# When VectorE scales the attention probabilities: behind the next projection's work, or ahead of it

## The reference

```python
def joint_softmax(parts, sink=None):
    ...
    es = [jnp.exp(s - m) for s in parts]
    den = es[0].sum(axis=-1, keepdims=True)
    ...
    if sink is not None:
        den = den + jnp.exp(sink - m)
    return [e / den for e in es]
```

```python
    hx = modulate(rmsnorm(x, g_pre_mix[l]), sh1, sc1)
    hc = modulate(rmsnorm(h_ctx, g_pre_mix[l]), csh1, csc1)
    y_x, y_c = mixer_sublayer(hx, hc, cos, sin, w_in[l], ...)
```

## Time and profile before

| | us |
|---|---|
| median of 3 runs | 2631.29 |
| lowest and highest | 2630.23, 2636.59 |
| the profiled execution's own time | 2638.48 |
| its span, first to last instruction | 2636.4 |
| PE busy | 2415.6 |
| DVE busy | 1743.0 |
| ACT busy | 1343.1 |
| mixer of layer 0, about | 37 to 740 |
| dense feed-forward, about | 740 to 1175 |
| mixer of layer 1, about | 1190 to 1560 |
| experts | from 1605 |

### The profile page before, as it was taken

How to read it: one execution, slowest core, us unless ns; L and a number is a source line. 1 busy time by engine, 2 the same in 40 slices (tenths; PEclk the granted TensorE clock), 3 DMA queues, 4 the chain that set the end, 5 groups by cost and what they waited for, 6 DMA issues and landing times.

```text
span 2636.4 us, 34852 instructions
## 1 busy us (share of the span) xinstructions
PE 2415.6 (92%) x12536; PEld 1970.1 (75%) x12536; DVE 1743.0 (66%) x2249; ACT 1343.1 (51%) x1636; POOL 28.1 (1%) x26
## 2 busy tenths in 40 slices
PE   6887899989889999987998978999999999999997
PEld 3666687667658788766887867787888888888885
DVE  5455434544275425547736638989989898989897
ACT  5334423433244323324534436777767676767675
POOL 0000010000000000000001000000000000000000
PEclk8988999989989999999999978999999999999999
DMA  5222132233324434322233436989899998989894
GB/s 218 80 80 96 69 107 89 88 106 119 112 80 159 143 112 160 135 88 79 98 104 118 152 127 264 357 337 361 338 353 343 353 338 337 361 329 365 327 366 171
DMA packets 128776, 528.62 MB, mean 201 GB/s; under 512 B 9136, under 2 KB 68016, under 8 KB 75440
## 3 DMA queue, kind: packets, MB, share of 16 engines
q1 hardware_dynamic: 126096, 520.86, 53.8%
q10 hardware_dynamic: 2592, 6.55, 0.8%
HBM read 526.33 MB, written 1.05 MB: 200 GB/s over the span
## 4 chain that ended last, share of the span: by engine, by line
PE 82%; DVE 10%; ACT 4%; issue 3%; DMA 1%; ACTq 0%; DVEq 0%; SPq 0%
PE O L1620 11%; PE pp L1277 9%; PE pp L1278 8%; PE pp L1279 8%; PE S L1598 8%; PE S L1596 8%; PE S L1597 8%; PE pp L1301 3%; DVE wsp L834 3%; PE O L1294 2%; PE T L1384 2%; ACT wsp L548 2%; PE S L1277 1%; PE S L1278 1%; PE T L1278 1%
## 5 line engine op out<-in xcount | busy, mean ns | idle before, releaser
L834 DVE TENSOR_TENSOR wsp<-raw,wsp 128x1024 fp32r<-128x1024 f32 (+3 forms) x344 | 379.4, 1127 | 523.0 <-ACT wsp L548 518.4
L1224 DVE TENSOR_TENSOR opr<-M,opr 128x2048 fp32r<-128x2048 f32 x168 | 383.5, 2287 | 31.1 <-ACT opr L782 28.3
L548 ACT ACTIVATE wsp<-raw 128x1024 fp32r<-128x1024 f32 (+3 forms) x344 | 322.5, 966 | 130.7 <-PE T L1279 82.3
L782 ACT ACTIVATE opr<-M 128x2048 fp32r<-128x2048 f32 x168 | 322.6, 1920 | 93.3 <-PE O L1620 52.0
L1596 PE MATMUL S<-opr,hx 128*128 128x512 f32 x896 | 359.5, 401 | 2.2 <-DVE hx L1229 2.2
L1598 PE MATMUL S<-opr,hx 128*128 128x512 f32 x896 | 350.7, 391 | 0.0
L1597 PE MATMUL S<-opr,hx 128*128 128x512 f32 x896 | 349.9, 391 | 0.0
L1620 PE MATMUL O<-opr,wsp 128*128 128x512 f32 x1344 | 311.3, 391 | 13.0 <-DVE opr L1224 13.0
L1277 PE MATMUL pp<-hx,wsp 128*128 128x512 f32 (+1 forms) x800 | 290.8, 363 | 35.4 <-DVE hx L916 14.8
L1620 PEld LDWEIGHTS O<-opr,wsp 128*128 128x128 f32 x1344 | 250.5, 188 | 67.6 <-DVE opr L1224 16.4
L1278 PE MATMUL pp<-hx,wsp 128*128 128x512 f32 (+1 forms) x800 | 283.5, 354 | 0.0
(11 more groups left out here) (203 smaller groups left out, 3422.6 us busy)
## 6 DMA issues: line engine op xcount, KB each, us to landing
M<-in_w_moe SPq DMA_DIRECT2D x168, 1024.0 KB, 4.9
raw<-in_w_main SPq DMA_DIRECT2D x132, 1024.0 KB, 4.9
raw<-in_w_moe SPq DMA_DIRECT2D x114, 1024.0 KB, 5.0
xm<-in_w_moe SPq DMA_DIRECT2D x56, 1024.0 KB, 5.7
raw<-in_w_br SPq DMA_DIRECT2D x24, 512.0 KB, 3.5
raw<-in_w_dn SPq DMA_DIRECT2D x8, 768.0 KB, 4.1
raw<-in_w_dn SPq DMA_DIRECT2D x8, 640.0 KB, 3.9
M<-in_rpb_rows ACTq DMA_DIRECT2D x16, 256.0 KB, 2.9
```

What stands on the lines that cost most here:

```text
L548: act.activation(wsp[:, slot, 0, 0:w], raw[:, slot // 2, half * w:half * w + w], ACT.Copy).then_inc(hi_done, 1)
L782: act.activation(wse[i % SPLIT_E][:, 0, :, :], raw_e[i % RAW_E], ACT.Copy).then_inc(e_hi, 1)
L834: dve.tensor_tensor(wsp[:, slot, 1, 0:w], raw[:, slot // 2, half * w:half * w + w], wsp[:, slot, 0, 0:w], ALU.subtract).then_inc(lo_done, 1)
L1224: dve.tensor_tensor(w[:, 1, :, :], raw_e[i % RAW_E], w[:, 0, :, :], ALU.subtract).then_inc(e_lo, 1)
```

## The change

The scaling of a pair's probabilities leaves `attn` and becomes a function of its own, `scale_probs`. Each row gets an entry `scale`, the slots of the row before it. DVE scales these at the very start of the row, ahead of the row's own slot and its projection work. So pair `s` is scaled one row behind its scores instead of at slot `s+1`, two or three rows behind. The wait for `exp_done` moves along with it. The other engines' code is the same.

```diff
-                rows.append(dict(slots=slots, what=what, i=i, u=gu, t=t, bank=bank, use=use[bank], l=l))
+                rows.append(dict(slots=slots, scale=rows[-1]["slots"] if rows else [], what=what, i=i, u=gu, t=t, bank=bank,
+                                 use=use[bank], l=l))
...
-            def attn(l, b, s):
+            def scale_probs(l, b, s):
                 units = attn_units(l)
-                nqt = (TOK if l == 0 else SEQ) // P
                 for half in range(2):
-                    n = 2 * (s - 1) + half
-                    if 0 <= n < len(units):
+                    n = 2 * s + half
+                    if n < len(units):
                         w = unit_base[l, b] + n
...
                         dve.tensor_scalar(pr[:, half, 0:N], pr[:, half, 0:N], sc[:, 4:5], None, ALU.mult).then_inc(probs_done, 1)
+
+            def attn(l, b, s):
+                units = attn_units(l)
+                nqt = (TOK if l == 0 else SEQ) // P
                 for half in range(2):
                     n = 2 * s + half
...
                 for row in mixer_steps[l]:
+                    for b, s in row["scale"]:
+                        scale_probs(l, b, s)
                     for b, s in row["slots"]:
                         attn(l, b, s)
```

## The result

| | before | after |
|---|---|---|
| median, us | 2630.76 | 2550.35 |
| lowest and highest of four runs | 2628.4 to 2636.59 | 2547.25 to 2555.97 |
| the profiled execution's own time | 2638.48 | 2547.89 |
| its span | 2636.4 | 2545.8 |

The ratio is 0.9694, with a 95% interval of 0.9669 to 0.9719: 80.4 us faster. The forecast was 2545 us and the range 2532 to 2586, so the direction and the size are right, and the time is 5.4 us above the forecast.

The account below looks back on a forecast made before the run. PE bounds the kernel, so its waits for scaled probabilities, 68.9 us, count. Gains with clock, 15.5 + 24.1 + 27.8 + 2.5 + 16.8 = 86.7 us, off the 2631.3 median gave 2545 us; range 2532 to 2586.

Parts of the forecast that it names:

- D: Layer 1's first attention: 2.5 us won of 6.9 us of gaps, the rest returning as waits for splits.
- Nothing changes: Rival: each gap returns one for one in front of a projection, 2631 us; chance 0.05.
- slower: Rival: the scaling in its new place holds up splits the PE wants next, for all 48 pairs, 2649 us; chance 0.03.
- the clock does not come back: Rival: the 17.3 us of clock gains fail to appear, 2562 us; chance 0.14.
- B: Second part of layer 0's first attention: four gaps 15.3, waits inside transposes 2.0, clock 6.8; 24.1 us won.
- the gap moves: Rival: C and E behave like D, winning 12.2 us instead of 44.6, 2577 us; chance 0.14.
- C: Layer 0's second attention: 17.0 of 21.3 us of gaps, two staying in part, plus 4.0 and clock 6.8; 27.8 us.
- E: Layer 1's second attention: all 12.6 us of gaps, 2.2 inside transposes and 2 of clock; 16.8 us won.
- inner gap: Second wait inside a pair's eight transposes, 1.97 us against 1.10, expected to go: 0.5 us each in B and C.
- A: First attention of layer 0, beside convolution and gate rows: 5.8 first gap, 2.7 second, 7.0 five other pairs; 15.5 us.
- clock terms: Slow PE clock behind gaps: 1.7 us won per gap over 2 us that goes entirely; 17.3 us in all.
- the loop: In D, maxima, exponential, splits, scaling and convolution form a cycle longer than PE's work per pair, limiting the gain to 0–6.9 us.

Follow-up runs that it names:

- e2: Changed kernel with the scaling moved only for the second attention of each layer, the first keeping the old place; 2591.70 us, ratio to before 0.9861.
- e3: Changed kernel plus one more VectorE multiplication by 1.0 per unit in the new place, making a pair's scaling longer; 2571.66 us, ratio to before 0.978.
- e7: Kernel before, with eight unread 512-column matmuls ahead of the wait in 16 pairs with gaps of 2.1 us or longer; 2617.93 us, ratio 0.9949.
- e9: Kernel before, unchanged, run again for a second trace; 2631.44 us.
- e5: Changed kernel, but in branch-projection rows holding a slot the scaling goes directly behind the row's result, ahead of its ending splits; 2553.21 us.

## Why the prediction was right, and where it was off

**The bound.** PE's standing still decided, and the gaps went: 68.9 to 9.3 us, where under 12 was forecast, with what is left in the two places named (2.59 us at 341.39, 1.73 at 471.69, those of the earlier trace rows), one of 0.97 at 447.59, and in D. "Nothing changes" and "slower" are ruled out by the time, "the clock does not come back" (2562 us) by the 8.7 us of busy time that went in B, and "the gap moves" in C and E by e2, which has 38.5 us from these two stretches alone, where that rival had 12.2. A scaling that holds up later work, the mechanism of "slower", does show once a pair's scaling is a microsecond longer: e3 loses 21.3 us by it, in C, D and E. The strict order of VectorE's queue, on which it rests, agrees with the wait of L963 for the exponential (6.3 us). ScalarE's exponentials in C, whose later start was named as a sign of being wrong, start no later: counted from the start of C, each of the 32 starts at the same time or earlier than in the second trace of before, the last one by 22.5 us.

**B** (forecast 24.1, measured 23.0). The gaps hold, and 8.7 us of busy time went where 2.0 + 6.8 were forecast. But the 2.0 were read wrongly. I had taken the 1.97 us of eight transposes behind the gap of 3.55, against 1.10 elsewhere, as a second wait inside them. All eight are slow alike, without a pause, at a clock of 0.50. The transposes from 257.97, then those from 244.31 (L1384, duration of one in ns, shortest, median and longest):

```profile
L1384 PE MATMUL T<-ident,M x8: 421/421/477, 258.0 to 259.5; 128*128 128x128 f32 x8
```

```profile
L1384 PE MATMUL T<-ident,M x8: 272/273/332, 244.3 to 245.1; 128*128 128x128 f32 x8
```

So there the "inner gap" is the clock once more, and that 2.0 + 6.8 came out so close is in part luck. The 1.1 missing are the wait for a split at the branch's last rows (L1439, 1.1 us), which the sum had not. The granted clock has no step below 1 in B; e7 shows that PE's standing still was its cause.

**A** (15.5, measured 12.7 and 12.8). The first gap gave 6.1 (forecast 5.8), the second 2.7 up to the start of its projection (forecast 2.7), the other five 6.9 (forecast 7.0). What failed is one omission: I had written that "part of each vanished gap returns as a longer wait for L834", and counted that wait, but not that the clock falls behind it. The projection behind the wait of 3.56 us lost 2.9 us to it, which is the whole miss. The clock of A as a whole hardly rose, from 0.91 to 0.92: the slow clock moved from the gaps to the waits for splits. I had given clock terms to gaps that go and none to waits that grow.

**C** (27.8; measured 30.1 on the first trace of before, 24.6 on the second). The standing still is right: 17.0 forecast, 16.5 measured (26.3 to 9.8, against the second trace). The clock and the inner gaps, 10.8 forecast, gave 8.0 against the second trace and 13.8 against the first. Here the two gaps that stay were taken as keeping their slow clock, and in after they don't: behind 2.59 us at 341.39 the clock stays at 1.00 (timeline of PE, then the windows there).

```profile
341.39 1.25 PE L1390 MATMUL T<-ident,M 128*128 128x128 f32 x8 [2.59 <-DVE M L965]
```

```profile
340.00:344.00 4.00, 2.61 (x22) 2.04 (x23) 3.89 (x8) 1.19 (x2) 0.00 (x0) 1.00 0.48 135
344.00:348.00 4.00, 4.00 (x22) 3.31 (x20) 2.17 (x6) 2.06 (x6) 0.00 (x0) 1.00 0.77 266
```

In part that is chance: in e2, whose order in C is the same, the clock falls behind that wait (2.58 us there), and C is 1.7 us longer.

**D** (2.5, measured 2.3 and 1.3) held as a size; no run tested the loop that the scaling was said not to leave. That the rest would return there as waits for splits was wrong, since PE waits for none in D. It waits 4.0 us for the probabilities still. **E** (16.8, measured 16.6 and 15.3) held.

**The sum.** On the first trace of before, the five stretches gave 84.6 us where 86.7 were forecast. The sentence that failed is that "this execution lies 7.2 us above the median of the runs, 2631.3, and since the gain doesn't depend on that, I forecast 2631.3 - 86.7". It does depend on it: e9 finds that excess in C, D and E, where the change removes it, and clock terms sized on one execution were taken off the median of others. With the second trace the five stretches give 77.0. Against that stand 4.2 us in the router's stage that no step of mine had and that the change didn't reorder: 81.2, where the medians differ by 80.4. (The heads of the two traces differ by another 2.1 us.) So the time came out within 5.4 us of the forecast by two errors in opposite directions, about -9.7 and +4.2, and this closeness is luck; the direction, the places and the size to within a tenth are not.

**Other forecasts.** PE's wait for a split: 15 to 25 in A and D, measured 15.7, all of it in A. Busy time of PE: a fall of some 15 us, measured 40.4 (31.3 against the second trace, 2406.5). That was an error of reading: I had put the inner gaps (9 us) outside busy time, part of which was the clock (see B), and had not counted the head, the router's stage and the excess of the first trace. The rest from the experts on is unchanged.

## What to carry to other kernels

A small operation that another engine waits for belongs in the queue directly behind the work it depends on, ahead of work that is not yet due; what it costs there is decided by what stands behind it, so lengthen it once and see which stretches pay. Moving it still further ahead of such work (e5) won nothing here. When a wait goes, follow the next wait on the same chain: here splitting one half slab more ahead won a further 22 us, 9 of which the first change had lost to the late splits. Size clock terms on an execution that lies at the median, or take two traces, and give a growing wait its clock term as well as a shrinking one.

## What the runs showed of the hardware that was not expected

- The same instructions with the same waits differed by 4 to 7 us by the clock alone: C at 256.9 and 251.5 us with 26 us of standing still in both, and the router's stage at 126 or 130 to 132 with 31 us.
- A gap's length alone did not tell whether the clock falls. In after it fell behind a wait of 1.91 us (at 1213.27, in D) and did not behind 2.04 and 2.59 in C. Behind the same wait of 2.97 us it fell in the first trace of before and not in the second; and of two waits that filling had left at 1.49 us, it fell behind one (e7, at 300.53) and not behind the other (255.91).
- PE work that nobody needs, put into gaps, makes the whole faster: 13.5 us in before, for 128 additional matmuls.
